# Turning the probabilities before the new scores in a fused attention and projection loop

## The chip, the cores and the metric

The kernel runs on one core of a Trainium2 chip. The core has a matrix engine (TensorE; PE in the rows, its weight loads PEld), a vector engine (VectorE, DVE), an activation engine (ScalarE, ACT), GpSimd (POOL) and SyncE (SP). Each engine runs its own instructions strictly in the order in which they are written; engines meet through semaphores only. The metric is the device time of one execution in microseconds. It is compared over several plain runs, beside one profiled execution that gives the trace.

## The reference, cut to what matters

The program is a two-layer backbone over 512 latent tokens of width 2048. Layer 0 has windowed attention (12 query heads, 4 KV heads, head size 128, window 128, 256 context tokens and a sink logit per head) beside a Fourier mixing, both multiplied by a gate `silu(z)`; layer 1 is a pooling mixer. The change is in the attention of layer 0 alone:

```
s_win = einsum('bqkgd,bjkd->bkgqj', qn, kw) * scale       # queries of a block against its window
s_ctx = einsum('bqkgd,bjkd->bkgqj', qn, k_ctx) * scale    # and against the context
logits = concatenate([sink, s_ctx, where(valid, s_win, -inf)])
p = softmax(logits)
out = p_ctx @ v_ctx + p_win @ v_win
y = concatenate([out, fourier_mix(f, w_f)]) ;  x + gate * ((y * silu(z)) @ w_out)
```

## The kernel before, in words

The attention stage is one loop over the 4 KV heads (`attention(i)`, lines 1128 to 1144 on TensorE; ScalarE and VectorE have functions of the same name). In each turn of it the core does two things at once: the attention of the 3 query heads that share this KV head, over 4 blocks of 128 queries, and one column group of the gate projection `z`, which is dense matrix work and fills TensorE while the softmax is made elsewhere.

The attention has 12 steps, k = 0 to 11: step k is one head of one block (block k // 3, head k % 3). A head of a block goes through these stations:

1. `scores(i, k)` (L1086 to L1103) on TensorE: queries by window keys and by context keys, each product as three matmuls of split numbers (a rounded part `hi` and a remainder `lo`), masks and sink added by small matmuls. The scores lie in PSUM banks 4 and 5, for one head at a time. Since the next scores overwrite them, `scores(i, k)` waits until the exponential of step k-1 is done (L1092). Heads of blocks 1 and 2 (k = 3 to 8) have 641 columns, the others 513; below they are called wide and narrow.
2. VectorE: the row maximum (L788) and its negation (L790).
3. ScalarE: the exponential with its row sum (L485), into `probs[k % 2]`. The two buffers of `probs` are shown in the rows as `kvmem` and `tmp`.
4. VectorE: reciprocal (L810) and scaling (L812) of the probabilities.
5. `turn(i, k)` (L1105 to L1113) on TensorE: 4 or 5 transposes of 128x128 into PSUM, in one buffer (`turned_tiles`). It waits for the scaled probabilities (L1106), and for k = 3, 6, 9 also until the output of the block before has been read out (`y_done`, L1110), since the fifth tile shares a bank with it.
6. ScalarE copies the turned tiles into `pt_hi` (L481), VectorE makes the remainder `pt_lo` (L806).
7. After the three heads of a block, `attend(i, n)` (L1116 to L1126) multiplies them by the values, at steps 4, 7, 10 and 13 (`BLOCK_SLOTS`). It waits for the third `pt_lo` of the block.

In between stand the projection units: `unit(...)` is six matmuls of 512 columns (two row tiles of the weights by three split products, L927). A list written by hand, `BANK_STEPS`, gives two of them to each step and four to each of steps 12 and 13; in a block step one of them goes right behind `attend`, ahead of the scores. The order on VectorE and ScalarE is also written by hand, with numbers of steps: at steps 2, 4, 6, 8, 10, 12, 13 (`UNIT_SLOTS`) the next weight tile is rounded (L311) and its remainder made (L573), at steps 1, 4, 7 the next block's queries are split (L460, L768), and at steps 1, 3, 5, 7, 9, 11, 12, 13 VectorE adds a part of a product that has nothing to do with the attention (L583). VectorE's order in a step is: read out a finished block, maximum, weight remainder, query remainder, `pt_lo` of the head before, reciprocal and scaling, the part of the other product. ScalarE's is: weight rounding, queries, copy of the turned tiles of the head before, exponential.

At the end of a KV head VectorE multiplies the gate into the outputs (L669, L672) before it comes to the first maximum of the next one. After step 0 TensorE also sums a product of VectorE with eight one-column matmuls (`reduce`, L1142).

Of the kernel before, what the change touches and what calls it, by code (L numbers as in the profile page):

```python
# [36 lines left out]
STEPS = BLOCKS * GQA  # L37
# [67 lines left out]
def score_width(k):  # L105

    first, end = block_tiles(k // GQA)
    return (end - first) * P + CTX + 1
# [12 lines left out]
def build(nc, weights, modb, xT, ctxT, vectors, wf, ident_in, identb_in, masks_in, rope_in, dft_tok_in,  # L121
          dft_ch_in, edges_in, outT):
    with ExitStack() as whole:
# [801 lines left out]
        def _(pe):  # L925
# [25 lines left out]
            def unit(n, b, s, m, make=unit_bank, signal=None):  # L951

                if m == 0:
                    pe.wait_ge(lo_ready, n * HALVES + (s + 1))
                if s == 0 and not (isinstance(b, int) and b == 0):
                    pe.wait_ge(bank_free, b * GROUP + (m + 1 - GROUP))
                ins = make(s, m)
                if s == HALVES - 1:
                    ins.then_inc(bank_done, 1)
                elif m == GROUP - 1:  # L960
                    ins.then_inc(weights_used, 1)

            def reduce(cg):

                pe.wait_ge(acc_step, cg * KT + KT)
                if not (isinstance(cg, int) and cg == 0):
                    pe.wait_ge(red_free, cg)
                for m in range(GROUP):
                    ins = mm(ps[:, RED_BANK, RED_COL + m:RED_COL + m + 1], modacc[:, m * P:(m + 1) * P], ones[:, 0:1],
                             m == 0, True)  # L970
                ins.then_inc(acc_reduced, 1)
# [114 lines left out]
            def scores(i, k):  # L1086
                n, j = divmod(k, GQA)
                first, end = block_tiles(n)
                if j == 0:
                    pe.wait_ge(piece_ready, i * PIECES + (PIECES_BEFORE if n == 0 else 5 + n))  # L1090
                if k:
                    pe.wait_ge(exp_done, i * STEPS + k)  # L1092
                qh, ql = q_hi[:, n % 2, j], q_lo[:, n % 2, j]
                at, window, past = 512 - (end - first) * P, slice(first * P, end * P), slice(SEQ, SEQ + CTX)
                three(ps[:, 4, at:512], qh, ql, k_hi[:, window], k_lo[:, window], True, False)
                if n > first:
                    mm(ps[:, 4, at:at + P], identb, masks[:, 0], False, False)
                if end > n + 1:
                    mm(ps[:, 4, 512 - P:512], identb, masks[:, 1], False, True)
                three(ps[:, 5, 0:CTX], qh, ql, k_hi[:, past], k_lo[:, past], True, True)  # L1100
                head = i * GQA + j
                mm(ps[:, 5, CTX:CTX + 2], ones_r[:], sink_hi[:, head], False, False)
                mm(ps[:, 5, CTX:CTX + 2], ones_r[:], sink_lo[:, head], False, True).then_inc(scores_done, 1)  # L1103

            def turn(i, k):  # L1105
                pe.wait_ge(probs_ready, i * STEPS + (k + 1))  # L1106
                if k == 0:
                    pe.wait_ge(red_free, i + M_Z)
                elif k % GQA == 0:
                    pe.wait_ge(y_done, i * BLOCKS + k // GQA)  # L1110
                for t in range(score_width(k) // P):
                    ins = nc.tensor.transpose(ps_flat[:, 6 * 512 + t * P:6 * 512 + (t + 1) * P],  # L1112
                                              probs[k % 2][:, t * P:(t + 1) * P], ident)  # L1113
                ins.then_inc(turned, 1)

            def attend(i, n):  # L1116

                first, end = block_tiles(n)
                tiles = list(range(first, end)) + [BLOCKS, BLOCKS + 1]
                pe.wait_ge(pt_ready, i * STEPS + GQA * (n + 1))  # L1120
                if n == 0:
                    pe.wait_ge(piece_ready, i * PIECES + 5)
                for c, t in enumerate(tiles):
                    ins = three(ps[:, 7, P:512], v_hi[:, t], v_lo[:, t], pt_hi[:, c], pt_lo[:, c], c == 0,
                                c == len(tiles) - 1)
                ins.then_inc(pv_done, 1)  # L1126

            def attention(i):
                step = 0
                for k, count in enumerate(BANK_STEPS):  # L1130
                    if k in BLOCK_SLOTS:
                        attend(i, BLOCK_SLOTS.index(k))
                        unit(i + G_Z, i + B_Z, *divmod(step, GROUP))
                        step, count = step + 1, count - 1
                    if k < STEPS:
                        scores(i, k)
                    if 0 < k <= STEPS:
                        turn(i, k - 1)
                    for _ in range(count):
                        unit(i + G_Z, i + B_Z, *divmod(step, GROUP))  # L1140
                        step += 1
                    if k == 0:  # L1142
                        reduce(i + (M_Z - 1))
                pe.wait_ge(y_done, i * BLOCKS + BLOCKS)

            with pe.Fori(0, KV_HEADS) as i:
                attention(i)
# [125 lines left out]
```

## Time and profile before

| | us |
|---|---|
| plain runs, median of 3 | 1699.92 (1699.41 to 1700.33) |
| profiled execution | 1703.19 |
| its span | 1701.3 |
| TensorE busy | 1537.1 (90%) |
| VectorE busy | 923.5 (54%) |
| ScalarE busy | 577.3 (34%) |
| attention stage, by the trace | about 545 to 860 |
| TensorE busy in it | 305.45 of 315 |

The rows of a timeline give the start of an instruction from the start of the span, its duration, engine, line of the code, operation, output and inputs, and in square brackets how long the engine was idle before it and what ended this. Matmuls overlap, so that the distance of two starts is shorter than the duration of one; TensorE's order and pace are read from the starts. Nearly all matmuls carry line 927, the helper's; the transposes have L1112. The granted clock is 1.00 at 2.4 GHz and 0.50 at 1.2 GHz.

### The profile page before, as it was taken

How to read it: one execution, taken by the hardware profiler on the slowest of the kernel's cores; microseconds unless marked ns; L12 is line 12 of the kernel's file. 1: busy time of each engine (PE TensorE's matmuls, PEld its weight loads, DVE VectorE, ACT ScalarE, POOL GpSimd, SP SyncE). 2: the span in 40 equal slices, each digit the busy share in tenths (PEclk: the TensorE clock that was granted, in tenths of full speed). 3: DMA queues.
4: the chain of work that ended last, by engine and by line, in shares of the span. 5: the costliest groups of instructions: out<-in, count | busy, mean ns of one | idle time of the engine just before them, and what ended most of it. 6: DMA issues, size and time to landing. Idle time of an engine off the chain costs nothing.

```text
span 1701.3 us, 19913 instructions
## 1 busy us (share of the span) xinstructions
PE 1537.1 (90%) x6988; PEld 1223.4 (72%) x6988; DVE 923.5 (54%) x1283; ACT 577.3 (34%) x806; POOL 71.0 (4%) x136
## 2 busy tenths in 40 slices
PE   3976799999999999999979999499999999989994
PEld 1434688877785888888857887388877788878883
DVE  3677653455553777767756555823448333353335
ACT  3765241244422343433332222322225222242221
POOL 0000000000010000000001000000000000000000
PEclk9997899999999999999989999699999999999997
DMA  9776234645463233323255555123223333223222
GB/s 326 268 255 205 91 108 145 221 162 172 149 200 101 87 115 95 123 86 123 86 185 197 185 191 182 46 88 99 93 92 112 136 99 99 97 76 99 92 81 99
DMA packets 68039, 232.47 MB, mean 137 GB/s; under 512 B 7328, under 2 KB 10400, under 8 KB 67872
## 3 DMA queue, kind: packets, MB, share of 16 engines
q1 hardware_dynamic: 42624, 151.01, 26.8%
q0 software_dynamic: 19520, 71.31, 12.8%
q10 hardware_dynamic: 5856, 9.63, 1.6%
q8 instruction: 24, 0.39, 0.1%
q14 instruction: 15, 0.12, 0.0%
HBM read 227.73 MB, written 4.19 MB: 136 GB/s over the span
## 4 chain that ended last, share of the span: by engine, by line
PE 71%; DVE 15%; DMA 5%; issue 4%; ACT 3%; ACTq 1%; DVEq 0%; POOL 0%; SPq 0%; POOLq 0%
PE ps L927 70%; DMA raw<-in_weights 3%; DVE w_lo L573 2%; DMA modchunk<-in_modb 2%; ACT tmp L411 1%; PE ps L1112 1%; DVE h_lo L633 1%; DVE scratch L583 1%; DVE w_lo L695 1%; DVE stat L788 1%; DVE tmp L669 1%; DVE tmp L624 1%; DVE tmp L866 1%; DVE main L624 1%; DVE h_lo L631 1%
## 5 line engine op out<-in xcount | busy, mean ns | idle before, releaser
L927 PE MATMUL ps<-h_hi,w_hi 128*128 128x512 f32 x1600 | 641.4, 401 | 70.3 <-DVE w_lo L573 41.9
L927 PE MATMUL ps<-h_lo,w_hi 128*128 128x512 f32 x1600 | 632.0, 395 | 0.0
L927 PE MATMUL ps<-h_hi,w_lo 128*128 128x512 f32 x1600 | 631.9, 395 | 0.0
L573 DVE TENSOR_TENSOR w_lo<-raw,w_hi 128x1024 fp32r<-128x1024 f32 x214 | 261.7, 1223 | 528.5 <-ACT w_hi L311 528.1
L311 ACT CAST w_hi<-raw 128x1024 fp32r<-128x1024 f32 x214 | 224.6, 1052 | 765.6 <-PE ps L927 765.4
L927 PEld LDWEIGHTS ps<-h_hi,w_hi 128*128 128x128 f32 x1600 | 306.6, 192 | 137.3 <-issue 35.9
L927 PEld LDWEIGHTS ps<-h_hi,w_lo 128*128 128x128 f32 x1600 | 306.0, 191 | 66.0
L927 PEld LDWEIGHTS ps<-h_lo,w_hi 128*128 128x128 f32 x1600 | 307.0, 192 | 60.1
L583 DVE SCALAR_TENSOR_TENSOR scratch<-modchunk,cond,scratch 128x512 f32<-128x512 f32 x240 | 179.8, 749 | 25.0 <-DMA modchunk<-in_modb 19.8
L280 POOL DMA_DIRECT2D modchunk<-in_modb x128 | 67.8, 530 | 1227.5 <-DVE scratch L583 1072.6
L481 ACT CAST pt_hi<-ps 128x512 fp32r<-128x512 f32 (+1 forms) x48 | 30.7, 639 | 121.2 <-PE ps L1112 121.2
L927 PE MATMUL ps<-w_hi,cond_split 128*4 128x512 f32 x64 | 33.3, 521 | 27.2 <-DVE w_lo L695 27.2
L788 DVE TENSOR_REDUCE stat<-ps 128x1 f32<-128x513 f32 (+1 forms) x48 | 36.3, 756 | 36.7 <-PE ps L927 36.5
L695 DVE TENSOR_TENSOR w_lo<-raw,w_hi 128x1024 fp32r<-128x1024 f32 x34 | 41.4, 1224 | 18.1 <-ACT w_hi L363 17.8
L695 DVE TENSOR_TENSOR h_lo<-raw,h_hi 128x1024 fp32r<-128x1024 f32 x32 | 38.9, 1222 | 22.7 <-ACT h_hi L363 22.4
L927 PE MATMUL ps<-k_hi,q_hi 128*128 128x256 f32 (+1 forms) x96 | 34.6, 360 | 10.1 <-ACT kvmem L485 5.7
L363 ACT CAST w_hi<-raw 128x1024 fp32r<-128x1024 f32 x34 | 35.4, 1045 | 17.7 <-DMA raw<-in_weights 15.7
L806 DVE TENSOR_TENSOR pt_lo<-ps,pt_hi 128x512 fp32r<-128x512 f32 (+1 forms) x48 | 36.1, 753 | 8.1 <-ACT pt_hi L481 7.5
L927 PE MATMUL ps<-h_hi,cond_split 128*4 128x512 f32 x64 | 31.8, 497 | 8.3 <-DVE h_lo L695 8.2
L363 ACT CAST h_hi<-raw 128x1024 fp32r<-128x1024 f32 x32 | 33.3, 1043 | 17.4 <-DMA raw<-in_weights 11.1
L927 PEld LDWEIGHTS ps<-w_hi,cond_split 128*4 128x4 f32 x64 | 5.9, 92 | 39.3 <-issue 30.7
L927 PEld LDWEIGHTS ps<-k_hi,q_hi 128*128 128x128 f32 x96 | 18.8, 196 | 17.4 <-ACT kvmem L485 9.3
(157 smaller groups left out, 1566.3 us busy)
## 6 DMA issues: line engine op xcount, KB each, us to landing
raw<-in_weights SPq DMA_DIRECT2D x280, 512.0 KB, 3.4
modchunk<-in_modb POOLq DMA_DIRECT2D x128, 512.0 KB, 3.7
main<-in_xT ACTq DMA_DIRECT2D x4, 1024.0 KB, 13.9
main<-in_xT POOLq DMA_DIRECT2D x4, 1024.0 KB, 9.9
out<-main SPq DMA_DIRECT2D x16, 256.0 KB, 2.3
kvmem<-in_ctxT ACTq DMA_DIRECT2D x1, 2048.0 KB, 17.5
dft_tok<-in_dft_tok ACTq DMA_DIRECT2D x1, 2048.0 KB, 11.6
kvmem<-in_rope ACTq DMA_DIRECT2D x1, 512.0 KB, 16.1
```

The source lines that it names most:

```text
L280: pool.dma_start(modchunk[:, slot].rearrange("p a n -> p (a n)"), src).then_inc(chunk_landed[slot], 16)
L311: nc.scalar.copy(w_hi[:, j % 2], raw[:, slot]).then_inc(hi_ready, 1)
L363: nc.scalar.copy(mod_hi[j % RAW_SLOTS], raw[:, j % RAW_SLOTS]).then_inc(hi_ready, 1)
L411: ins = nc.scalar.activation(tmp[q:q + 32, m % 2, 0:SEQ], view(m)[p:p + 32], ACT.Identity)
L481: nc.scalar.copy(*turned_tiles(k - 1, pt_hi)).then_inc(pt_hi_ready, 1)
L573: nc.vector.tensor_tensor(w_lo[:, j % 2], raw[:, j % RAW_SLOTS], w_hi[:, j % 2].bitcast(F32), ALU.subtract).then_inc(lo_ready, 1)
L583: ins = nc.vector.scalar_tensor_tensor(out=modacc[:], in0=modchunk[:, s % 2, r], scalar=cond[:, kt, 0:1], in1=modacc[:], op0=ALU.mult, op1 ...
L624: nc.vector.scalar_tensor_tensor(out=dst, in0=x, scalar=g, in1=r, op0=ALU.mult, op1=ALU.mult).then_inc(tile_ready, 1)
L695: nc.vector.tensor_tensor(mod_lo[j % RAW_SLOTS], raw[:, j % RAW_SLOTS], mod_hi[j % RAW_SLOTS].bitcast(F32), ALU.subtract).then_inc(lo_read ...
L788: chain.link(nc.vector.tensor_reduce(stat[:, 0, par:par + 1], ps_flat[:, S_END - width:S_END], AX.X, ALU.max))
L806: nc.vector.tensor_tensor(lo_part, turned_part, hi_part.bitcast(F32), ALU.subtract).then_inc(pt_ready, 1)
L927: return nc.tensor.matmul(out, lhsT, rhs, start=start, stop=stop, skip_group_check=True)
```

## The change

In each step of the loop on TensorE, the transposes of the head one step back stand ahead of the scores of the new head. Before, they stood behind them. Nothing else is touched: all other engines have the same instructions in the same order.

```diff
                         attend(i, BLOCK_SLOTS.index(k))
                         unit(i + G_Z, i + B_Z, *divmod(step, GROUP))
                         step, count = step + 1, count - 1
+                    if 0 < k <= STEPS:
+                        turn(i, k - 1)
                     if k < STEPS:
                         scores(i, k)
-                    if 0 < k <= STEPS:
-                        turn(i, k - 1)
                     for _ in range(count):
                         unit(i + G_Z, i + B_Z, *divmod(step, GROUP))
                         step += 1
```

TensorE's order from the summing products behind step 0 to the first matmuls of step 1 (`ones_r,scratch` are the summing products, `k_hi,q_hi` begins the scores, L1112 are the transposes, the rows without a tile are the waits of L1092 and L1106):

```order
 L965 ISA
 L927 MATMUL ps<-ones_r,scratch 128x1 x4
-L1092 ISA
+L1106 ISA
+L1112 MATMUL ps<-kvmem 128x128 x4
 L927 MATMUL ps<-k_hi,q_hi 128x256
 L927 MATMUL ps<-k_lo,q_hi 128x256
```

The first thing behind the summing products is now the turn of head 0, with its wait for the scaled probabilities.

TensorE's order in the kernel before from the end of the scores of the block step 4 to the start of step 5:

```order
L927 MATMUL ps<-sink_lo,ones_r 128x2
L1110 ISA
L1112 MATMUL ps<-kvmem,tmp 128x128 x5
L927 MATMUL ps<-h_hi,w_hi 128x512
L927 MATMUL ps<-h_lo,w_hi 128x512
L927 MATMUL ps<-h_hi,w_lo 128x512
L927 MATMUL ps<-h_hi,w_hi 128x512
L927 MATMUL ps<-h_lo,w_hi 128x512
L927 MATMUL ps<-h_hi,w_lo 128x512
L1092 REGISTER_ALU
L927 MATMUL ps<-k_hi,q_hi 128x384
```

The same place in the changed kernel:

```order
L927 MATMUL ps<-sink_lo,ones_r 128x2
L927 MATMUL ps<-h_hi,w_hi 128x512
L927 MATMUL ps<-h_lo,w_hi 128x512
L927 MATMUL ps<-h_hi,w_lo 128x512
L927 MATMUL ps<-h_hi,w_hi 128x512
L927 MATMUL ps<-h_lo,w_hi 128x512
L927 MATMUL ps<-h_hi,w_lo 128x512
L1106 REGISTER_ALU
L1112 MATMUL ps<-kvmem 128x128 x5
L927 MATMUL ps<-k_hi,q_hi 128x384
```

The scores of head 4 are now followed by six matmuls (one unit) and then by the turn of head 4 itself. Before, the turn of head 3, the unit and the scores of head 5 (two to three times as many instructions) stood between them. The wait of L1092 is no longer in the new order as an instruction of its own, since the wait for the probabilities comes later than the exponential in any case.

## Rows read from the trace of the kernel before

**Rows 1.** The page: busy time of TensorE (part 1) and the chain (part 4).
```profile
PE 1537.1 (90%) x6988; PEld 1223.4 (72%) x6988; DVE 923.5 (54%) x1283; ACT 577.3 (34%) x806; POOL 71.0 (4%) x136
...
PE 71%; DVE 15%; DMA 5%; issue 4%; ACT 3%; ACTq 1%; DVEq 0%; POOL 0%; SPq 0%; POOLq 0%
```

**Rows 2.** Waits of TensorE, 545 to 860 us: total us, times, longest.
```profile
PE ps L927 <- ACT kvmem L485: 5.7, 7, 1.7
PE ps L927 <- DVE q_lo L768: 3.6, 1, 3.6
PE ps L1112 <- DVE kvmem L812: 2.9, 8, 0.5
PE ps L927 <- ACT tmp L485: 0.7, 4, 0.2
```

**Rows 3.** Timeline, third KV head, step 4: start us, us, engine, line, op, [idle before].
```profile
728.15 0.34 PE L927 MATMUL ps<-k_hi,q_hi 128*128 128x384 f32 x1
...
729.35 0.77 PE L1112 MATMUL ps<-kvmem,tmp 128*128 128x128 f32 x5
729.52 0.83 DVE L788 TENSOR_REDUCE stat<-ps 128x1 f32<-128x641 f32 x1 [1.88 <-PE ps L927]
...
730.48 1.23 DVE L573 TENSOR_TENSOR w_lo<-raw,w_hi 128x1024 fp32r<-128x1024 f32 x1
...
730.74 0.80 ACT L485 ACTIVATE kvmem<-ps,stat 128x641 f32<-128x641 f32 x1
...
731.62 0.55 DVE L768 TENSOR_TENSOR q_lo<-main,q_hi 128x384 fp32r<-128x384 f32 x1
...
731.68 0.45 PE L927 MATMUL ps<-k_hi,q_hi 128*128 128x384 f32 x1 [0.19 <-ACT kvmem L485]
...
732.09 0.82 DVE L806 TENSOR_TENSOR pt_lo<-ps,pt_hi 128x640 fp32r<-128x640 f32 x1
...
732.83 0.15 DVE L810 RECIPROCAL stat<-stat 128x1 f32<-128x1 f32 x1
...
733.01 0.55 DVE L812 TENSOR_SCALAR kvmem<-kvmem,stat 128x640 f32<-128x640 f32 x1
...
733.62 0.77 PE L1112 MATMUL ps<-kvmem 128*128 128x128 f32 x5 [0.49 <-DVE kvmem L812]
```

**Rows 4.** Timeline of TensorE at the end of step 11, third KV head.
```profile
768.60 0.40 PE L927 MATMUL ps<-h_hi,w_hi 128*128 128x512 f32 x1
...
769.98 0.60 PE L1112 MATMUL ps<-kvmem,tmp 128*128 128x128 f32 x4
```

**Rows 5.** Timeline at the turn from the second to the third KV head.
```profile
708.34 0.68 DVE L788 TENSOR_REDUCE stat<-ps 128x1 f32<-128x513 f32 x1
...
709.31 1.03 DVE L768 TENSOR_TENSOR v_lo<-kvmem,v_hi 128x512 fp32r<-128x512 f32 x2
...
710.08 0.39 PE L927 MATMUL ps<-k_hi,q_hi 128*128 128x256 f32 x1 [1.66 <-ACT kvmem L485]
...
710.51 0.49 DVE L812 TENSOR_SCALAR kvmem<-kvmem,stat 128x512 f32<-128x512 f32 x1
```

**Rows 6.** Groups by shape, 545 to 860 us: remainder of the narrow turned tiles.
```profile
L806 DVE TENSOR_TENSOR pt_lo<-ps,pt_hi 128x512 fp32r<-128x512 f32 x24 | 16.5, 686 | 2.9 <-ACT pt_hi L481 2.3
```

**Rows 7.** Windows of 1 us: TensorE busy, granted clock (PEclk), DMA share, GB/s.
```profile
709.00:710.00 1.00, 0.00 (x0) 1.00 0.53 74
711.00:712.00 1.00, 1.00 (x7) 0.50 0.29 115
791.00:792.00 1.00, 1.00 (x8) 1.00 0.12 45
```

**Rows 8.** Timeline of TensorE, fourth KV head: scores(1) and turn(11).
```profile
789.86 0.39 PE L927 MATMUL ps<-k_hi,q_hi 128*128 128x256 f32 x1 [1.67 <-ACT kvmem L485]
...
847.96 0.60 PE L1112 MATMUL ps<-kvmem,tmp 128*128 128x128 f32 x4
```

**Rows 9.** Waits, 545 to 860 us: the one of VectorE on ScalarE's copy.
```profile
DVE pt_lo L806 <- ACT pt_hi L481: 7.5, 12, 0.7
```

## The prediction

> **What bounds the kernel now.** I read the page first: TensorE is busy for 90% of the span and carries 71% of the chain that ended last [rows 1]. So whatever makes TensorE stand still is paid in full, unless it stood still there already. Next I read TensorE's waits in the attention stage, 545 to 860 us [rows 2]. They are small: 5.7 + 3.6 + 2.9 + 0.7 = 12.9 us in 20 occasions. 3.6 us of them is the one wait before the first head; three of 1.66 us stand at the turn from one KV head to the next (one is in rows 5). About 4.3 us is left for the four KV heads, 1.1 us each. The trace counts such a wait from the modelled end of the last matmul, which comes about 0.2 us after the next one could have been issued, so that some six small waits of a KV head cost about 2.5 us of issue time. I use that number.
>
> Then I followed one head through all engines, head 4 of the third KV head [rows 3], which is the hardest place. TensorE begins its scores at 728.15 and would issue the next thing at 729.35. VectorE takes the row maximum at 729.52, makes a weight remainder (730.48) and a query remainder (731.62) that stand in its order, then the remainder of the previous head's turned probabilities (732.09), the reciprocal (732.83) and the normalised probabilities (733.01 to 733.56). ScalarE's exponential (730.74) lies beside this and is not the last. TensorE turns head 4 at 733.62. **From the issue end of the scores to the turn this chain is 733.62 - 729.35 = 4.27 us.** VectorE's work, not ScalarE's, makes it long.
>
> **What the change does to that.** No instruction is added or removed; the order on TensorE alone changes. Before, scores(k) were followed by turn(k-1), the projection units, scores(k+1) and only then turn(k), so the chain above had the units, one turn and the next scores as cover. Now scores(k) are followed by the units and then by turn(k). The cover loses a turn (0.52 us for five tiles) and a whole set of scores (729.35 - 728.15 = 1.20 us [rows 3]; about 0.2 less for narrow heads). Behind the waiting turn stand the new head's scores, which needed only the exponential and are now held by the probabilities too, and behind them the units, which need neither. TensorE's order is fixed, so nothing fills the hole.
>
> One unit of six matmuls takes 769.98 - 768.60 = 1.38 us to issue [rows 4]. So wait = chain - cover, with a cover of 2.76 us where two units stand between and 1.38 us behind the block steps 4, 7 and 10, whose other unit goes ahead of the scores. Step by step, in one KV head:
>
> - Turn 4: chain 4.27, cover 1.38: **2.9 us**. Before, turn, unit and scores covered 0.52 + 1.38 + 1.20 = 3.1, and 1.17 was waited, which the trace names 0.19 and 0.49 [rows 3].
> - Turn 7: the same without the weight remainder (731.62 - 730.48 = 1.14): 3.13 - 1.38 = **1.75 us**.
> - Turn 10: without the query remainder (732.09 - 731.62 = 0.47) and for a narrow row, where maximum, remainder (686 ns [rows 6] against 0.82 us [rows 3]) and scaling (0.49 against 0.55 [rows 3, 5]) are together 0.33 shorter: 3.47 - 1.38 = **2.1 us**.
> - Turn 8: 4.27 - 0.47 = 3.80, cover 2.76: **1.05 us**. Turn 2, the narrow case: 3.47 - 2.76 = **0.7 us**.
> - Turn 5 and turn 1 have no remainders of weights in their way; there the exponential is last: 0.17 to the maximum, about 1.05 for it and its negation, 731.68 - 730.74 = 0.94 for the exponential until it is seen, 733.01 - 732.83 = 0.18, 0.55 and 0.06 [rows 3], 2.95 in all, cover 2.76: **0.2 us**, and 0.05 for the narrow turn 1.
> - The attention product of block 1 needs head 5's remainder, which VectorE makes behind a maximum and a weight remainder: 732.91 - 729.35 - 0.47 = 3.09, and 0.06 to be seen, against 2.76: **0.4 us**.
> - Turns 3, 6 and 9 have an attention product as extra cover, turn 11 only the narrow exponential chain: nothing.
>
> Sum 2.9 + 1.75 + 2.1 + 1.05 + 0.7 + 0.25 + 0.4 = 9.15 us where 2.5 was waited: +6.65 us in each KV head.
>
> **At the turn between KV heads** TensorE waits before and after. Its release was the exponential of head 0: scores(1) start at 710.08 after 1.66 us. Now turn(0) comes first and needs the probabilities: VectorE, late from the gating of the KV head before, starts the maximum at 708.34, makes the value remainders (709.31) and ends the scaling at 711.00 [rows 5]. With 0.06 to be seen that is 711.06, so +0.98 us each time. The first KV head has no late VectorE but the same order, and I give it the same. Together 7.6 us per KV head, **4 x 7.6 = +30.5 us**.
>
> What could come back: the query loads, weight casts and the background products on VectorE lie beside this; their work is unchanged and they follow TensorE's pace. SyncE's and GpSimd's transfers ask for their slots later, which costs nothing. ScalarE gets the turned tiles earlier, while the scores run. That frees it for the exponential some 0.2 us earlier, which the formula counts only where the exponential is last. Bounds of this term: at least +4 x (1.75 + 2.9 + 2.1 - 2.5) = +17 us if the small waits are all absorbed, at most +40 us if each of the 13 releases costs 0.2 us more.
>
> **The clock.** A second price is TensorE's own speed. At the turn into the third KV head the granted clock was 1.00 in the idle microsecond and 0.50 (1.2 GHz of 2.4) after it, at 711 us; at the next turn, after the same wait, it stayed at 1.00 [rows 7]. From scores(1) to turn(11) the KV head with the fall took 769.98 - 710.08 = 59.90 us and the one without 847.96 - 789.86 = 58.10 us [rows 4, 5, 8]: one fall costs up to 1.8 us. Before, it fell in 2 of 3 turns after about 2.6 us with nothing but one-column products and waiting. Now the turn has 3.9 us of this and the transposes, turn 4 about 3.4 (wait and turn), turn 10 2.5 and turn 7 2.3. I give falls to the first two nearly always and to the others half the time: 2.7 per KV head where 0.7 were, 2 more, at 1.2 us each, since a slow stretch also covers part of the next small wait. That is 4 x 2 x 1.2 = **+10 us**. Ends: 0, and 31 us (every KV head with 4.3 falls more at the full 1.8).
>
> The Trainium skill has a rule against this term ("TensorE: Matmul & The Clock Gate", "Why this matters for your kernels"): only gaps between bursts that are longer than any of my waits put the clock down. By it the term is 0 and the sum ends at +30.5. The trace does not agree: the clock fell after a gap of 1.66 us, so I keep the term. The same page ("Part 4: PE-mode transpose") says that transposes don't count as busy work for the clock; by it the transposes, now directly behind each wait, lengthen the quiet stretch. No run here shows that yet.
>
> **The sum** is made against the profiled execution: span 1701.3 + 30.5 + 10 = 1741.8, with the 1.9 us around it 1743.7. The median of the plain runs stands 3.3 us below the profiled one, so **1740 us**.
>
> **Rivals.**
> - *Only the waits, no more falls of the clock*: 1699.9 + 30.5 = 1730. For it: one turn of three kept its clock. Against it: two did not. Chance 0.22.
> - *The clock falls after nearly every wait of over 1 us*: turns 0, 4, 7, 8 and 10, at the full price: 1699.9 + 30.5 + 31 = 1761. For it: the fall after 1.66 us, and that half the speed makes the scores ahead of the next chain later. Against it: before, 0.49 us at turn 4 brought no fall, and the units run dense in between. Chance 0.18.
> - *Half of the waits are absorbed*, since VectorE idles between steps and could run ahead: about +17, 1717. Against it: the chain begins with the scores, which nothing lets start earlier. Chance 0.06.
> - *Not slower*: the earlier turn takes ScalarE's copy and VectorE's remainder out of the chain of the new head. Before, the exponential of head 4 stood behind that copy (it starts at 730.74, its maximum was ready by about 730.5), and VectorE waits 12 times, 7.5 us in all, for the copy [rows 9]. If this waiting were what bounds the steps, 7.5 us would come back: 1692. The point from which it decides is a chain shorter than its cover, under 1.38 us behind a block step; it is 4.27. Chance 0.03.
> - *My forecast*, 1740 (own range 1732 to 1750): chance 0.51.
>
> The order of the instructions shows that the change does what it says, so that is no rival.
>
> **Range.** 1723 to 1762 leaves out the half-absorbed case and the extreme of the clock. Slower or faster by over 0.2%, 3.4 us, is what can be told from no change here: faster 0.04, within 0.03, slower 0.93.
>
> **What would show it.** In TensorE's waits the releaser of the transposes (VectorE's scaled probabilities) should go from 2.9 us to some 40 us in the stage, with single waits of 2.5 to 3 us behind the block steps, and the wait for the exponential should vanish. ScalarE's idle time for the transposes stays large but costs nothing. The time from one KV head to the next should go from 79.8 us to about 90. The clock row should show 6 to 10 more stretches at 0.50. It would be wrong if the wait at turn 4 were under 2 us, or if the stage grew while TensorE's waits did not.

## The result

The changed kernel takes 1745.37 us (median of 4 runs, 1741.62 to 1747.47), the kernel before 1700.12 us beside it. The ratio is 1.0248, 95% interval 1.0223 to 1.0273: 42 us or 2.5% slower (38 to 46 us; the two medians lie 45 us apart). The forecast was 1740 us with a range of 1723 to 1762. The profiled execution took 1744.56 us with a span of 1742.7, where the working had 1743.7 and 1741.8.

TensorE's work is the same, 6988 matmuls, and its share of the span falls by a point [rows 1]. Its busy time grows by 15 us all the same, at a mean granted clock of 0.947 against 0.958 before. Page of the changed kernel, busy time and chain:

```profile
PE 1552.3 (89%) x6988; PEld 1233.6 (71%) x6988; DVE 923.5 (53%) x1283; ACT 580.0 (33%) x806; POOL 71.3 (4%) x136
...
PE 72%; DVE 16%; issue 4%; DMA 3%; ACT 3%; ACTq 1%; DVEq 0%; POOL 0%; SPq 0%; POOLq 0%
```

TensorE's waits in the attention stage of the changed kernel (total us, times, longest); they answer to [rows 2]:

```profile
PE ps L1112 <- DVE kvmem L812: 31.8, 20, 2.6
PE ps L1112 <- DVE tmp L812: 6.3, 4, 1.6
PE ps L927 <- DVE pt_lo L806: 0.5, 3, 0.2
```

The wait for the exponential is gone. In its place stands the wait of the transposes for the scaled probabilities, 38.1 us in 24 occasions, where all of TensorE's waits after the first head were 9.3 us before. The forecast was some 40.

The same head as in [rows 3], step 4 of the third KV head, in the changed kernel. The first row is the first matmul behind the scores, the last row the turn (start us, us, engine, line, operation):

```profile
753.90 0.48 PE L927 MATMUL ps<-h_hi,w_hi 128*128 128x512 f32 x1
...
754.08 0.82 DVE L788 TENSOR_REDUCE stat<-ps 128x1 f32<-128x641 f32 x1 [2.42 <-PE ps L927]
...
755.03 1.23 DVE L573 TENSOR_TENSOR w_lo<-raw,w_hi 128x1024 fp32r<-128x1024 f32 x1
755.12 0.80 ACT L485 ACTIVATE kvmem<-ps,stat 128x641 f32<-128x641 f32 x1 [1.53 <-DVE stat L790]
...
756.18 0.55 DVE L768 TENSOR_TENSOR q_lo<-main,q_hi 128x384 fp32r<-128x384 f32 x1
...
756.65 0.82 DVE L806 TENSOR_TENSOR pt_lo<-ps,pt_hi 128x640 fp32r<-128x640 f32 x1
757.38 0.15 DVE L810 RECIPROCAL stat<-stat 128x1 f32<-128x1 f32 x1
757.57 0.55 DVE L812 TENSOR_SCALAR kvmem<-kvmem,stat 128x640 f32<-128x640 f32 x1
...
758.17 0.70 PE L1112 MATMUL ps<-kvmem 128*128 128x128 f32 x3 [2.63 <-DVE kvmem L812]
```

The chain from the issue end of the scores to the turn is 758.17 - 753.90 = 4.27 us, to the digit what it was before. The copy of the previous head's tiles is now done earlier and no longer holds up the exponential, and the exponential did start a little earlier behind its scores (755.12 - 753.90 = 1.22 against 730.74 - 729.35 = 1.39). It gained nothing, because the two remainders of VectorE (755.03, 756.18) end after it. Under this chain there is now one unit of 1.38 us, and TensorE stands still for 2.9 us by issue, 2.63 by the trace's count.

The turn from the second to the third KV head, which answers to [rows 5]:

```profile
729.67 0.68 DVE L788 TENSOR_REDUCE stat<-ps 128x1 f32<-128x513 f32 x1
...
730.64 1.02 DVE L768 TENSOR_TENSOR v_lo<-kvmem,v_hi 128x512 fp32r<-128x512 f32 x2
...
731.84 0.49 DVE L812 TENSOR_SCALAR kvmem<-kvmem,stat 128x512 f32<-128x512 f32 x1
...
732.38 0.90 PE L1112 MATMUL ps<-kvmem 128*128 128x128 f32 x3 [2.64 <-DVE kvmem L812]
```

The distance from the maximum to the turn is 732.38 - 729.67 = 2.71 us; before, the maximum released the scores after 710.08 - 708.34 = 1.74. That is +0.97, as worked out (0.98). From one turn of head 0 to the next the changed kernel takes 90.7 and 89.9 us, where scores(1) came every 79.8 before.

The clock behind turn 4, windows of 3 us (busy, granted clock, DMA share, GB/s); TensorE was quiet in the first and dense in the second:

```profile
756.00:759.00 3.00, 0.83 (x6) 0.91 0.46 150
759.00:762.00 3.00, 3.00 (x14) 0.52 0.06 25
```

TensorE does dense work in the second window at a granted clock of 0.52. From the first scores to the end of the last attention product, kernel before and then changed kernel:

```profile
544.85:856.12 311.27, 301.72 (x1665) 0.98 0.32 101
```

```profile
543.59:898.27 354.68, 315.98 (x1665) 0.94 0.27 89
```

The stage has 1665 matmul records in both and takes 354.68 - 311.27 = 43.4 us longer; the span 41.4 us. So the whole loss lies in the stage. In the records of the granted clock I counted stretches of 3.4 us at 1.2 GHz within it, leaving aside the low clock with which it begins: 2 before, 10 now. Four lie behind turn 0, four behind turn 4, one behind turn 10, and one of those at turn 0 is followed by a second.

### The profile page after: what moved, and what is told of

Its sections match the earlier page's. It is cut to its first block, busy times and chain, and to the rows that moved or that the text cites. A ratio compares the mean times of both kernels' runs of the same rounds, so it can differ in the third digit from the quotient of the medians.

```text
span 1742.7 us, 19925 instructions
## 1 busy us (share of the span) xinstructions
PE 1552.3 (89%) x6988; PEld 1233.6 (71%) x6988; DVE 923.5 (53%) x1283; ACT 580.0 (33%) x806; POOL 71.3 (4%) x136
## 4 chain that ended last, share of the span: by engine, by line
PE 72%; DVE 16%; issue 4%; DMA 3%; ACT 3%; ACTq 1%; DVEq 0%; POOL 0%; SPq 0%; POOLq 0%
PE ps L927 70%; DMA raw<-in_weights 2%; DVE w_lo L573 2%; PE ps L1112 2%; ACT tmp L411 1%; DVE stat L788 1%; DMA modchunk<-in_modb 1%; DVE h_lo L633 1%; DVE pt_lo L806 1%; DVE scratch L583 1%; DVE w_lo L695 1%; DVE tmp L669 1%; DVE tmp L624 1%; DVE tmp L866 1%; DVE main L624 1%
## 5 line engine op out<-in xcount | busy, mean ns | idle before, releaser
L1112 PE MATMUL ps<-kvmem 128*128 128x128 f32 x108 | 19.1, 310 | 31.8 <-DVE kvmem L812 31.8
L927 PE MATMUL ps<-k_hi,q_hi 128*128 128x256 f32 (+1 forms) x96 | 38.9, 406 | 3.6 <-DVE q_lo L768 3.6
L1112 PEld LDWEIGHTS ps<-kvmem 128*128 128x128 f32 x108 | 13.1, 153 | 39.5 <-DVE kvmem L812 39.0
L363 ACT CAST h_hi<-raw 128x1024 fp32r<-128x1024 f32 x32 | 33.3, 1043 | 17.1 <-DMA raw<-in_weights 16.5
L927 PE MATMUL ps<-h_hi,cond_split 128*4 128x512 f32 x64 | 31.4, 491 | 7.3 <-DVE h_lo L695 7.1
L806 DVE TENSOR_TENSOR pt_lo<-ps,pt_hi 128x512 fp32r<-128x512 f32 (+1 forms) x48 | 36.0, 750 | 0.0
## 6 DMA issues: line engine op xcount, KB each, us to landing
kvmem<-in_ctxT ACTq DMA_DIRECT2D x1, 2048.0 KB, 17.5
```

The lines of the kernel that those rows point to most:

```text
L363: nc.scalar.copy(mod_hi[j % RAW_SLOTS], raw[:, j % RAW_SLOTS]).then_inc(hi_ready, 1)
L806: nc.vector.tensor_tensor(lo_part, turned_part, hi_part.bitcast(F32), ALU.subtract).then_inc(pt_ready, 1)
L927: return nc.tensor.matmul(out, lhsT, rhs, start=start, stop=stop, skip_group_check=True)
```

## The experiments

Times are medians of a kernel's runs. Each ratio is to the kernel before on the same chip, whose median was 1701.72 us beside the four kernels with the turn first in some steps, 1701.27 beside the next four and 1703.91 beside the last three. So the ratios are compared, not the distances of the medians from 1700.12. "Stage" is the profiled time from the first scores to the end of the last attention product, and "slow" the number of 3.4 us stretches at 1.2 GHz in it, counted as above.

| kernel | median us | ratio (95% interval) | stage us | slow |
|---|---|---|---|---|
| before | 1700.12 | 1 | 311.27 | 2 |
| changed | 1745.37 | 1.0248 (1.0223 to 1.0273) | 354.68 | 10 |
| turn first in step 1 | 1710.79 | 1.0060 (1.0043 to 1.0077) | 319.04 | 6 |
| turn first in 5, 8, 11 | 1718.53 | 1.0097 (1.0077 to 1.0118) | 328.76 | 5 |
| turn first in 4, 7, 10 | 1705.71 | 1.0020 (1.0004 to 1.0036) | 316.58 | 2 |
| turn first in 2, 3, 6, 9, 12 | 1710.47 | 1.0054 (1.0037 to 1.0071) | 320.82 | 3 |
| changed + matmuls of zeros | 1733.96 | 1.0187 (1.0164 to 1.0211) | 341.45 | 1 |
| changed + remainders behind | 1714.93 | 1.0075 (1.0058 to 1.0092) | 330.50 | 6 |
| changed + units behind | 1730.95 | 1.0165 (1.0144 to 1.0186) | 342.88 | 6 |
| before + units behind | 1692.91 | 0.9944 (0.9922 to 0.9966) | 301.22 | 2 |
| before + units behind, one moved | 1682.14 | 0.9864 (0.9839 to 0.9890) | 294.17 | 0 |
| changed + all three | 1703.99 | 0.9998 (0.9985 to 1.0011) | 314.39 | 1 |
| before + remainders behind | 1695.69 | 0.9956 (0.9936 to 0.9976) | 309.58 | 4 |

**The change in four parts.** The steps in which the turn stands first are a set S; the four kernels have S = (1,), (5, 8, 11), (4, 7, 10) and (2, 3, 6, 9, 12), which together are the change. The edit is to the kernel before.

```diff
+                    first = k in S
+                    if first:
+                        turn(i, k - 1)
                     if k < STEPS:
                         scores(i, k)
-                    if 0 < k <= STEPS:
+                    if 0 < k <= STEPS and not first:
                         turn(i, k - 1)
```

Step 1:

> The turn stands ahead of the scores in step 1 of each KV head alone; all other steps are as before. Theory (waits by chain minus cover, plus falls of the clock): the turn of head 0 waits about 2.6 us where scores(1) waited 1.66, so +1.0 us per KV head, +4 us, and the clock falls at every turn between KV heads, two more falls of some 1.5 us: about 1707 us. Rival (only the waits cost): 1704. Rival (this place costs nothing, VectorE's lateness is paid anyway): 1700.

```profile
629.97 1.11 PE L1112 MATMUL ps<-kvmem 128*128 128x128 f32 x4 [2.66 <-DVE kvmem L812]
```

Measured +10 us (0.60% of 1700); the stage of the profiled execution, the fastest of the four, grew by 7.8. The row is the turn of head 0 at the second KV head; it waits 2.66 us where the scores waited 1.66 before. The waits of that size explain 4 us. The rest goes with four more slow stretches, more than the two I expected, because at three turns the clock stayed down for two stretches, not one. The rivals (1700 and 1704) lie below the interval, 1707 to 1713.

Steps 5, 8 and 11:

> The turn stands first in steps 5, 8 and 11 alone, the ones behind the block steps. Theory: the covers of turns 4, 7 and 10 lose the scores but keep the turn before, so they wait 2.4, 1.3 and 1.7 us, +2.8 us per KV head by the same sum, +11 us, and the clock falls behind turn 4 in some KV heads (0 to 4 falls of 1.5 us): 1711 to 1717 us. Rival (the wait is due to the place of the turn ahead of the block's own scores, not to the lost cover): 1701.

Measured 1718.5 us, in the stage +17.5 with three more slow stretches. The median lies 1.5 us above the forecast's upper end, while the ratio makes +16.5 us, which is just inside. In the first KV head the trace names waits of 2.12, 1.09 and 1.43 us for turns 4, 7 and 10, each some 0.25 below the 2.4, 1.3 and 1.7 worked out by issue. The clock fell behind turn 4 in two KV heads, and at all three turns between KV heads instead of two. The rival (1701) falls: of the four parts, the steps behind the block steps cost most.

Steps 4, 7 and 10:

> The turn stands first in the block steps 4, 7 and 10 alone. Theory: turns 4, 7 and 10 lose 0.5 us of cover each and scores 5, 8 and 11 wait for the exponential earlier, +1.45 us per KV head, +6 us: 1706 us, no new falls of the clock. Rival (the block steps hold most of the loss, through the wait for the block's read-out ahead of turns 3, 6 and 9): 1715 or more, with a named wait on the read-out.

```profile
PE ps L927 <- ACT kvmem L485: 8.2, 11, 1.7
...
PE ps L1112 <- DVE kvmem L812: 4.7, 11, 0.7
PE ps L927 <- ACT tmp L485: 2.2, 4, 0.6
```

Measured 1705.7 us, stage +5.3 (5.8 expected), no new slow stretch. The waits (total us, times, longest) are those for the exponential and for the probabilities, and the read-out of a block is not among them. The rival falls.

The remaining steps:

> The turn stands first in steps 2, 3, 6, 9 and 12 alone. Theory: turn 2 waits 0.7 us, turn 8 1.3 where 0.3 were, the attention product of block 1 0.4: +2.1 us per KV head, +8.5 us: 1709 us, no new falls of the clock. Rival (steps with two units behind them cover the chain): 1700.

Measured 1710.5 us, stage +9.6. The theory of the waits holds (+8.5 us expected), but for one more slow stretch, where none was expected.

The four ratios add up to +2.31%, 39 us, against 42 for the whole. The parts' new slow stretches are 4 + 3 + 0 + 1 = 8, as many as the whole change has, though not all at the same places. What is missing in the sum lies within the intervals.

**The clock by itself.** Matmuls that add zeros to a bank which is being summed anyway fill the quiet stretch ahead of turns 0 and 4.

```diff
+                    if k in (1, 5):
+                        for _ in range(9):
+                            mm(ps[0:HEADS, 0], sink_hi[:, :, 1], h_hi[:, 0], False, False)
                     if 0 < k <= STEPS:
                         turn(i, k - 1)
```

> The changed kernel with nine matmuls of zeros (12 zero columns times 512 columns of h, added to PSUM bank 0, which changes nothing) put ahead of the turn in steps 1 and 5. They take some 2.1 us, less than the 2.6 us that TensorE waits there anyway. Theory (the rest above the waits is the clock, which falls because TensorE is quiet there): the waits stay, by issue, as they are, and the falls behind turns 0 and 4 go, 8 of the 10 slow stretches of the stage: 12 us less than the changed kernel, about 1733 us. Rival (the falls cost nothing beside the waits, or come from elsewhere): 1745, with fewer falls or as many. Rival (work added to TensorE costs its time): 1760 or more.

The first matmul behind the scores of step 4, the nine matmuls and the turn behind them, third KV head:

```profile
745.33 0.48 PE L927 MATMUL ps<-h_hi,w_hi 128*128 128x512 f32 x1
...
746.81 2.25 PE L927 MATMUL ps<-h_hi,sink_hi 128*12 128x512 f32 x9
749.61 0.77 PE L1112 MATMUL ps<-kvmem 128*128 128x128 f32 x5 [0.56 <-DVE kvmem L812]
```

The granted clock across this place, and the stage as a whole:

```profile
747.00:750.00 3.00, 2.44 (x13) 1.00 0.35 87
750.00:753.00 3.00, 3.00 (x21) 1.00 0.21 87
```

```profile
543.81:885.26 341.45, 318.50 (x1737) 0.99 0.27 92
```

The turn still comes 749.61 - 745.33 = 4.28 us after the issue end of the scores (4.27 without the zeros), after 0.56 us of waiting where it had been 2.63, and the clock stays at 1.00. One slow stretch is left of ten. The stage is 354.68 - 341.45 = 13.2 us shorter although TensorE has 72 matmuls more, and the median fell by 0.61% or 10 us (12 expected). So a slow stretch cost 13.2 / 9 = 1.5 us. That leaves out the low clock with which each stage begins: it lasts 6.8 us in the changed kernel and 3.4 here, and with that difference counted as a tenth stretch the price is 1.3 us. Within this one kernel the price can be read from whole KV heads, here by the start of the summing products in the second, third and fourth:

```profile
634.80 0.95 PE L927 MATMUL ps<-ones_r,scratch 128*128 128x1 f32 x8
...
722.62 0.95 PE L927 MATMUL ps<-ones_r,scratch 128*128 128x1 f32 x8
...
808.87 0.95 PE L927 MATMUL ps<-ones_r,scratch 128*128 128x1 f32 x8
```

The first distance, 87.82 us, holds the one slow stretch, the second, 86.25 us, none: 1.57 us. I take 1.3 to 1.6 us. Against the kernel before, this kernel's stage is 341.45 - 311.27 = 30.2 us longer with one slow stretch fewer, so that the waits alone make some 31.7 us of the loss. Both rivals fall.

**The chain.** VectorE makes its two remainders behind the scaling of the probabilities:

```diff
-                    if k in UNIT_SLOTS:
-                        lo(i + G_Z, UNIT_SLOTS.index(k) + 2)
-                    if k in QUERY_SLOTS:
-                        ...
                     if 1 <= k <= STEPS:
                         ...
                     if k < STEPS:
                         ...
                         nc.vector.tensor_scalar(p, p, stat[:, 3, par:par + 1], None,
                                                 ALU.mult).then_inc(probs_ready, 1)
+                    if k in UNIT_SLOTS:
+                        lo(i + G_Z, UNIT_SLOTS.index(k) + 2)
+                    if k in QUERY_SLOTS:
+                        ...
```

> The changed kernel, and VectorE makes the weight remainder and the query remainder of a step behind the scaling of the probabilities, not ahead of it. Theory (VectorE's chain sets the waits): the chain to turn 4 falls from 4.27 to about 2.9 us, turn 2 and the attention product stop waiting, 4.3 us less in each KV head, -17 us, and with a shorter quiet stretch the clock stops falling at turn 4, -6 us: about 1722 us. Rival (ScalarE's exponential or the semaphores set the chain, the remainders fill gaps of VectorE): 1745.

Step 4 of the third KV head; L806 is the scaling in this kernel, L800 the remainder of the turned tiles:

```profile
743.04 0.82 DVE L788 TENSOR_REDUCE stat<-ps 128x1 f32<-128x641 f32 x1 [2.43 <-PE ps L927]
...
743.97 0.81 DVE L800 TENSOR_TENSOR pt_lo<-ps,pt_hi 128x640 fp32r<-128x640 f32 x1
744.09 0.80 ACT L485 ACTIVATE kvmem<-ps,stat 128x641 f32<-128x641 f32 x1 [1.53 <-DVE stat L790]
...
745.21 0.55 DVE L806 TENSOR_SCALAR kvmem<-kvmem,stat 128x640 f32<-128x640 f32 x1
...
745.82 0.76 PE L1112 MATMUL ps<-kvmem 128*128 128x128 f32 x5 [1.31 <-DVE kvmem L806]
```

The scaling now starts 745.21 - 743.04 = 2.17 us behind the maximum, where it was 757.57 - 754.08 = 3.49, and TensorE waits 1.31 us instead of 2.63. The stage is 24.2 us shorter (23 expected, waits and falls together), and no slow stretch lies behind turn 4 any more. The ratio fell by 1.73%, 29 us, so the gain is larger than forecast (1714.9 us measured, 1722 expected). The profiled execution shows less of it because it took 1723.52 us, while the four others took 1713.49 to 1715.93. What made it slower was not followed up; its mean granted clock was 0.951, theirs 0.956 to 0.958. The rival falls.

**The cover.** Both units of a block step behind the scores:

```diff
                         attend(i, BLOCK_SLOTS.index(k))
-                        unit(i + G_Z, i + B_Z, *divmod(step, GROUP))
-                        step, count = step + 1, count - 1
```

> The changed kernel, and in the block steps both units stand behind the scores. Theory: turns 4, 7 and 10 get 1.38 us more cover each, and turns 3, 6 and 9, now directly behind the attention product, wait 0.8 us for its read-out: -1.8 us in each KV head, -7 us, and fewer falls of the clock at turn 4, -6 us: about 1732 us. Rival (the cover is worth nothing, the wait moves with the unit): 1745.

```profile
PE ps L1112 <- DVE kvmem L812: 21.0, 20, 2.6
PE ps L1112 <- DVE main L782: 8.1, 12, 0.8
PE ps L927 <- DVE h_lo L631: 6.1, 1, 6.1
PE ps L927 <- DVE q_lo L768: 3.6, 1, 3.6
PE ps L1112 <- DVE tmp L812: 0.8, 3, 0.3
```

The rows of h_lo and q_lo lie behind the stage and ahead of the first head. Measured 1731.0 us (1732 expected), the stage 11.8 us shorter with four slow stretches fewer. The waits for the probabilities fell from 38.1 to 21.8 us, and 8.1 us of waiting for the block's read-out came in their place, 12 times, as expected.

The same in the order of before:

> The kernel before, and in the block steps both units stand behind the scores and the turn. Theory (wait is chain minus cover): the cover of turns 4, 7 and 10 grows by 1.38 us to 4.5 us against a chain of 4.27, so that all small waits of a KV head go, and turns 3, 6 and 9 have the scores as cover for the read-out: -2.7 us in each KV head, -11 us: 1690 us. Rival (the read-out or the third remainder ahead of the product is waited for instead): 1700 or more.

Measured 1692.9 us, stage -10.05 (1690 and -11 expected). Here the scores cover the read-out, and the trace names no wait inside a KV head. The theory holds, the rival falls.

**Can both be had?** In both orders one unit is moved from step 12 to step 0:

```diff
-BANK_STEPS = (2,) * STEPS + (4, 4)
+BANK_STEPS = (3,) + (2,) * (STEPS - 1) + (3, 4)
```

> The kernel before, both units behind the scores and the turn in the block steps, and one unit moved from step 12 to step 0 (3 units in step 0, 3 in step 12), so that it lies in the 1.66 us that TensorE waits at each turn between KV heads. Theory (that wait is VectorE's late maximum, and TensorE has a unit to put there): the wait falls to 0.3 us, 1.38 us less at three turns, and the two falls of the clock go: -7 us from the kernel with the units behind (1693), about 1686 us. Rival (the unit's PSUM bank is not free yet and TensorE waits for the gating instead): 1693.

All that TensorE waits for behind the first head, and the stage:

```profile
PE ps L927 <- ACT kvmem L485: 0.9, 3, 0.3
```

```profile
544.36:838.53 294.17, 293.25 (x1665) 0.99 0.32 107
```

1682.1 us, 1.36% faster than before and the fastest version here; TensorE is busy for 293.25 of 294.17 us of the stage, with no slow stretch. The stage is 301.22 - 294.17 = 7.05 us shorter than with the units behind alone, as expected. The whole gain is larger than forecast: the ratio makes it 23 us, where 1686 meant 14. The stage is 17.1 us shorter than before; the rest was not traced to a cause. The rival (1693) falls.

> The changed order with all three remedies: VectorE's remainders behind the scaling, both units behind the scores, one unit moved from step 12 to step 0. Theory: the turn of head 0 waits 1.2 us, turns 3, 6 and 9 wait 0.8 for the read-out, the others 0.2 each, 4.6 us per KV head where the kernel before has 4.4, no falls of the clock: 1699 us, no better than the order of before without remedies and 13 us behind that order with two of them. Rival (turning first is as good once the covers suffice): 1686.

```profile
PE ps L1112 <- DVE main L782: 8.1, 12, 0.8
...
PE ps L1112 <- DVE kvmem L806: 4.7, 4, 1.3
```

1704.0 us, the same as the kernel before (1 us less expected). The wait for the read-out, which the scores cover in the other order, and the one of turn 0 are the named waits that turning first keeps. It lies 22 us behind the other order with two of the remedies, where 13 were expected. Of the 20.2 us between the stages the named waits explain 12.8 - 0.9 = 11.9; with 0.26 us for each of 13 more waits, as at turn 4, and one slow stretch it is some 17, and the last 3 us are open. The rival (1686) falls.

> The kernel before, with VectorE's weight and query remainders behind the scaling. Theory: the chain to turns 4, 8 and 10 is shorter, the waits at the turns go and those for the exponential stay, -1.4 us per KV head, -5.6 us: 1695 us. In the changed kernel the same edit took about 30 us. Rival (the remainders behind the scaling hold up the next maximum and cost what they save): 1701.

1695.7 us, by the ratio 7.5 us less than before (5.6 expected); its interval, 4 to 11 us, leaves out the rival of no gain (1701). In the stage of the profiled execution, one of the two slowest of its ten, only 1.7 us came back, with four slow stretches at the same 1.66 us waits at which the kernel before had two.

## Why the prediction was right

- **What bounds.** TensorE's waits were what counted: 38.6 us are named after the first head where 9.3 were, in 27 occasions where 19 were. With the 0.26 us that the trace leaves out of such a wait (2.89 by issue against 2.63 at turn 4) that is an estimate of 29.3 + 8 x 0.26 = 31.4 us for the waits; the clock makes up the rest of the 43.4 us of the stage.
- **The chain against its cover.** Right, nearly to the digit. Turn 4: chain 4.27 as read off, wait by issue 2.9. Turn 7: 778.42 - 775.16 - 1.38 = 1.9 (1.75 worked out); turn 10: 797.29 - 793.82 - 1.38 = 2.1 (2.1), from the starts of unit and turn in the same trace. The waits in sum: some 31.7 us by the kernel with matmuls of zeros, 30.5 worked out. The working gave each KV head some six small waits before; the trace names 16 in all, four per KV head. The 2.5 us that it gave them is not far off even so: with the units behind, these waits went and the stage fell by 10.05 us, 2.5 per KV head.

```profile
775.16 0.48 PE L927 MATMUL ps<-h_hi,w_hi 128*128 128x512 f32 x1
...
778.42 0.77 PE L1112 MATMUL ps<-kvmem,tmp 128*128 128x128 f32 x5 [1.61 <-DVE tmp L812]
...
793.82 0.48 PE L927 MATMUL ps<-h_hi,w_hi 128*128 128x512 f32 x1
...
797.29 0.66 PE L1112 MATMUL ps<-kvmem 128*128 128x128 f32 x4 [1.83 <-DVE kvmem L812]
```

- **The turn between KV heads.** +0.97 measured, +0.98 worked out. For the first KV head it was shown as a wait of its own, 1.08 us in the trace.
- **What could come back** came to nothing, as said: at turn 4 an earlier copy and exponential lie under VectorE's remainders.
- **The clock.** The number of new slow stretches was right (8), their places less so: behind turns 0 and 4 always, as given; behind turn 7 never and behind turn 10 once in four, where I had given half; a second stretch at turn 0 made up for it. That the number came out is luck in part. The price was somewhat too low: 1.2 us each in the working, 1.3 to 1.6 by the matmuls of zeros, so 10 to 13 us for eight where 10 were given. With 31.4 for the waits and 8 x 1.5 for the clock the sum is 43.4 us, what the stage grew by (42 to 44 with the two ends of the price); the working had 40.5.
- **The last step.** The working meets the profiled execution (1743.7 and 1744.56 us) more closely than the median (1740 and 1745.37). The stage grew by 3 us more than worked out, and the rest of the span took 2 us less. The 3.3 us that were taken off for the median did not recur: here the profiled execution is 0.8 us below it.
- **The rivals.** *Only the waits* (1730) is what the matmuls of zeros come close to (1734) and falls for the change itself. *Nearly every wait*: behind turn 7 and turn 8 no fall at all. *Half absorbed* and *not slower* fall with the chain of 4.27.
- **The rule of the Trainium skill** on gaps ("TensorE: Matmul & The Clock Gate", "Why this matters for your kernels"), by which gaps as short as these cost no clock, does not hold here: gaps of 1.08 to 2.65 us were followed by 1.2 GHz, the shortest at the turn of head 0 in the first KV head of the changed kernel. It does not hold in the kernel before either when the one-column products ahead of the wait are taken as part of the gap: from their start to the scores it is 710.08 - 707.47 = 2.61 us. That transposes don't count as work for the clock (the same page, "Part 4: PE-mode transpose") was tried by no run. The row of the one-column products, ahead of the scores of [rows 5]:

```profile
707.47 0.95 PE L927 MATMUL ps<-ones_r,scratch 128*128 128x1 f32 x8
```

## What to carry to other kernels

Where two dependent chains share an in-order engine, the order of its pieces is a matter of cover: take the chain from the trace, from the issue end of the piece that starts it to the piece that needs it, subtract what is issued in between, and the rest is an estimate of the wait in another order, as long as the chain stays the same (4.27 us in both orders here). Then count the slow stretches apart: they differ between kernels with the same waits. Put the piece with the longest chain behind it (here the scores) as early as possible, and the one that only ends a chain late. And look at what the engine in the middle of the chain does first: two remainders that nobody was waiting for made up 1.3 us of 4.27.

## What the runs showed of the hardware

- A quiet stretch of TensorE costs twice: its own length and, when the clock falls, another 1.3 to 1.6 us for 3.4 us at 1.2 GHz. Work without any use, put into the quiet stretch, kept 2.4 GHz and made the kernel 0.6% faster.
- The same wait of 1.66 us at the same place was followed by a fall or not from one turn to the next: two of three in the kernel before, all three with VectorE's remainders moved, one of three with the units behind. At turn 4 waits of 2.1 us (turn first in 5, 8, 11) were followed by a fall in two of four KV heads and waits of 2.6 us (changed kernel) in all four. Where it falls isn't settled by the wait's length alone.
